# Hybrid decoder block on one core: tokens first in the load queue, lambda turned by TensorE, the order of the first tensor work changed

## The reference, cut to what matters

```python
def rms_norm(x, g):
    return x * lax.rsqrt(jnp.mean(x * x, -1, keepdims=True) + 1e-6) * g

h = jnp.concatenate([meta, x], axis=1)             # 272 x 1024
u = rms_norm(h, g_mix)
z = u @ w_in                                       # 1024 x 2048
c_val, c_gate, r_x, r_gate = jnp.split(z, 4, -1)   # 512 each
conv_out = conformer_conv_group(c_val, c_gate, ...)  # GLU, causal conv of 31 taps, LayerNorm, silu
lru_out = griffin_group(r_x, r_gate, ...)          # conv of 4 taps, RG-LRU, gelu gate
#   in rg_lru: log_a = -8 * r * softplus(-lam)     # lam: 512 values
h = h + concatenate([conv_out, lru_out]) @ w_out
u = rms_norm(h, g_ffn)
h = h + moe_ffn(u, ...)                            # 32 experts, top 4, clamped SwiGLU
out = rms_norm(h, g_final)[:, 16:]
```

## Time and profile before

| | us |
|---|---|
| median of 3 executions | 1006.41 |
| lowest, highest | 1006.39, 1010.56 |
| the profiled execution | 1006.83 |
| its span | 1005.0 |

### The profile page before, as it was taken

One profiled execution on the slowest core, in us unless ns is written; L12 is line 12 of the kernel. 1 busy time (PEld: TensorE's weight loads), 2 busy tenths in 40 slices (PEclk: granted clock), 3 DMA queues, 4 the chain that ended last, 5 costly groups with the idle time before them and its releaser, 6 DMA issues.

```text
span 1005.0 us, 11664 instructions
## 1 busy us (share of the span) xinstructions
PE 976.6 (97%) x4737; PEld 387.7 (39%) x4737; DVE 235.8 (23%) x624; ACT 163.0 (16%) x312; POOL 45.4 (5%) x89
## 2 busy tenths in 40 slices
PE   9999999999999999999999999999999999999996
PEld 7888433333343333333333333333333333333332
DVE  6986311112211111111111111111111111111121
ACT  5783211111101000111111101110011110100112
POOL 2860000000000000000000000000000000000000
PEclk9999999999999999999999999999999999999999
DMA  9999999999999999999999999999999999999995
GB/s 272 361 398 425 363 407 425 428 429 432 435 431 429 431 432 430 430 434 430 430 434 433 430 430 436 428 430 437 430 430 434 429 430 434 425 428 428 427 424 239
DMA packets 36802, 418.90 MB, mean 417 GB/s; under 512 B 5915, under 2 KB 16427, under 8 KB 19494
## 3 DMA queue, kind: packets, MB, share of 16 engines
q1 hardware_dynamic: 36038, 418.17, 98.9%
q10 hardware_dynamic: 736, 0.34, 0.1%
HBM read 417.45 MB, written 1.05 MB: 416 GB/s over the span
## 4 chain that ended last, share of the span: by engine, by line
PE 82%; DMA 14%; ACT 2%; another core or an unknown queue 1%; DVE 0%; issue 0%; SPq 0%; ACTq 0%; DVEq 0%
PE bank L1487 37%; PE bank L1532 19%; DMA gu_ring<-in_w_gate_up 10%; PE bank L1285 6%; PE bank L1459 5%; PE bank L1397 4%; DMA dn_ring<-in_w_down 4%; PE bank L1304 3%; PE bank L1391 3%; ACT reg L750 2%; PE bank L1508 1%; PE bank L1502 1%; PE bank L1224 0%; SPq L396 0%
## 5 line engine op out<-in xcount | busy, mean ns | idle before, releaser
L1487 PE MATMUL bank<-gu_ring,reg 128*64 128x512 f32 x2048 | 450.4, 595 | 11.1 <-DMA gu_ring<-in_w_gate_up 11.0
L1487 PEld LDWEIGHTS bank<-gu_ring,reg 128*64 128x64 f32 x2048 | 142.6, 137 | 310.1 <-issue 285.3
L1532 PE MATMUL bank<-dn_ring,reg 128*64 128x512 f32 x1024 | 227.4, 595 | 7.7 <-ACT reg L750 7.2
L1114 DVE TENSOR_SCALAR reg<-bank 128x256 f32<-128x256 f32 x64 | 24.2, 420 | 587.4 <-PE bank L1487 587.4
L1532 PEld LDWEIGHTS bank<-dn_ring,reg 128*64 128x64 f32 x1024 | 70.5, 137 | 143.0 <-issue 124.5
L745 ACT ACTIVATE reg<-reg 128x512 f32<-128x512 f32 x29 | 18.3, 630 | 456.4 <-DVE reg L1114 456.4
L1459 PE MATMUL bank<-reg 64*128 64x512 f32 x256 | 63.9, 616 | 0.9 <-DVE reg L1183 0.9
L1285 PE MATMUL bank<-dn_ring,gu_ring 128*128 128x272 f32 (+1 forms) x256 | 59.0, 390 | 0.3 <-ACT reg L612 0.3
L1397 PE MATMUL bank<-xh,reg 128*64 128x512 f32 x248 | 58.5, 592 | 0.0
L1285 PEld LDWEIGHTS bank<-dn_ring,gu_ring 128*128 128x128 f32 x256 | 48.4, 190 | 9.6 <-DMA gu_ring<-in_w_in 0.6
L752 ACT ACTIVATE reg<-bank 128x512 f32<-128x512 f32 x29 | 17.3, 597 | 208.4 <-PE bank L1532 208.4
(11 more groups left out here) (257 smaller groups left out, 424.7 us busy)
## 6 DMA issues: line engine op xcount, KB each, us to landing
gu_ring<-in_w_gate_up SPq DMA_DIRECT2D x46, 4096.0 KB, 33.0
dn_ring<-in_w_down SPq DMA_DIRECT2D x22, 4096.0 KB, 33.0
gu_ring<-in_w_gate_up SPq DMA_DIRECT2D x31, 2048.0 KB, 39.2
dn_ring<-in_w_down SPq DMA_DIRECT2D x10, 2048.0 KB, 20.3
dn_ring<-in_w_down SPq DMA_DIRECT2D x17, 1024.0 KB, 14.2
gu_ring<-in_w_gate_up SPq DMA_DIRECT2D x9, 1024.0 KB, 7.8
gu_ring<-in_w_in SPq DMA_DIRECT2D x6, 1024.0 KB, 12.3
dn_ring<-in_w_out SPq DMA_DIRECT2D x4, 1024.0 KB, 11.2
```

The lines of the kernel that those rows point to most:

```text
L1114: ins = V.tensor_scalar(half(xglu, b), glu_v[:, 0], 7.0, None, ALU.min)
L1487: ins = mm(gub[b][64 * h:64 * h + 64, :], xgT[:, j, :], of_half(gu_ring[:, s, j, 1024 * b:1024 * b + 1024], h), start=False, stop=(j == KD ...
L1532: ins = mm(out[64 * h:64 * h + 64, :], a[:, at:at + SLOTS], dn_ring[:, s, k, 512 * h:512 * h + 512], start=(i == 0), stop=(i == KD - 1))
```

## The change

SP no longer loads the identity: ACT does, as its first load, with a semaphore of its own. So the tokens are the first loads in SP's queue. `lam` is loaded as four rows of 128 into `grow`, which has 20 rows now, and is turned together with the gains; POOL reads its four columns from `colv` and waits for `g_ok`. PE issues six dummy products and not nine. It turns chunks 0 to 6 of the first token tile before it turns `grow`, and chunk 7 of the first tile and of the meta tokens just ahead of chunk 7 of the second tile. DVE squares the first token tile before it copies the turned gains. The two DVE operations for softplus go behind the eight `normed_x`. The vectors are turned after chunk 4 of `z_half(0, 0)` and not ahead of it, and chunk 0 of the first product waits for one DVE copy instead of two.

```diff
@@ -39,7 +39,7 @@
 
 V_CW, V_CB, V_LG, V_LB, V_LW, V_LCB, V_BA, V_BX = 0, 31, 32, 33, 34, 38, 39, 40
 NV = 41
-NG = 2 * KD
+NG = 2 * KD + CC
 GP = 4
 PK = KD // GP
 
@@ -134,7 +134,7 @@
         mixl = lnsq
         bdiag = xh[:, 0, :].rearrange("p (c n) -> p c n", c=2 * CC)
         prod = xh[:, 1, :].rearrange("p (i t) -> p i t", i=PROD)
-        lamc = tiny[:, 32:36]
+        lamc = colv[:, CC * NV + 2 * KD:CC * NV + NG]
         hsq = xh[:, :, :].rearrange("p b (d t) -> p (b d) t", d=4)
 
 
@@ -241,7 +241,7 @@
 
 
         x_in, meta_in = [sem("x_in0"), sem("x_in1")], sem("meta_in")
-        g_in, lam_in, vec_in, cst_in = sem("g_in"), sem("lam_in"), sem("vec_in"), sem("cst_in")
+        g_in, id_in, vec_in, cst_in = sem("g_in"), sem("id_in"), sem("vec_in"), sem("cst_in")
         tri_ok, selb_ok = sem("tri_ok"), sem("selb_ok")
         lruw_in, route_in, bgu_in = sem("lruw_in"), sem("route_in"), sem("bgu_in")
         win0_in, row3_in = sem("win0_in"), sem("row3_in")
@@ -333,7 +333,6 @@
         @block.sync
         def _(sp):
 
-            sp.dma_start(cst[:, C_ID:C_ID + P], const[:, C_ID:C_ID + P]).then_inc(g_in, 16)
             for t in range(TT):
                 sp.dma_start(xh[:, t, :], x[0, t * P:(t + 1) * P, :]).then_inc(x_in[t], 16)
             def win_single(p):
@@ -538,7 +537,7 @@
                 ins.then_inc(sp_pool, 1)
                 pool.wait_ge(sp_pool, done[0])
 
-            pool.wait_ge(lam_in, 16)
+            pool.wait_ge(g_ok, 1)
             after(G.tensor_scalar(spt[3], lamc, -1.0, 0.0, ALU.mult, ALU.max))
             after(G.tensor_scalar(spt[2], lamc, 0.0, None, ALU.max))
             after(G.tensor_tensor(spt[0], spt[3], spt[2], ALU.add))
@@ -593,10 +592,11 @@
         @block.scalar
         def _(act):
 
+            act.dma_start(cst[:, C_ID:C_ID + P], const[:, C_ID:C_ID + P]).then_inc(id_in, 16)
             act.dma_start(metah, meta).then_inc(meta_in, 16)
             for r, row in enumerate((g_mix, g_ffn)):
                 act.dma_start(grow[KD * r:KD * (r + 1), :], row[0].rearrange("(k n) -> k n", k=KD)).then_inc(g_in, 16)
-            act.dma_start(lamc, lam[0].rearrange("(c p) -> p c", p=P), allow_slow_non_contiguous=True).then_inc(lam_in, 16)
+            act.dma_start(grow[2 * KD:NG, :], lam[0].rearrange("(c n) -> c n", c=CC)).then_inc(g_in, 16)
 
             act.wait_ge(set_ok, 1)
             nc.scalar.activation(tiny[:, 38:39], one_col, ACT.Sqrt)
@@ -841,11 +841,11 @@
             V.memset(ssq[:, 2:3], 1.0).then_inc(set_ok, 1)
             v.wait_ge(set_ok, 1)
 
-            v.wait_ge(g_ps, 1)
-            V.tensor_copy(colv[:, CC * NV:], bank[7][:, 512 - NG:512]).then_inc(g_ok, 1)
             v.wait_ge(x_in[0], 16)
             V.tensor_tensor_reduce(out=sq_scr[:, 0:D], in0=xh[:, 0, :], in1=xh[:, 0, :], scale=1.0, scalar=0.0,
                                    op0=ALU.mult, op1=ALU.add, accum_out=ssq[:, 0:1]).then_inc(sq0_ok, 1)
+            v.wait_ge(g_ps, 1)
+            V.tensor_copy(colv[:, CC * NV:], bank[7][:, 512 - NG:512]).then_inc(g_ok, 1)
             def scaled_x(k):
                 v.wait_ge(xT_ps, k + 1)
                 V.tensor_scalar(xg[:, k, :], bank[k][:, 0:T], gcol(k), None, ALU.mult).then_inc(xT_dve, 1)
@@ -874,15 +874,15 @@
 
             v.wait_ge(rb_ps, 1)
             link(V.tensor_copy(rb, bank[3][:, 0:T]))
-            v.wait_ge(sp_act, 1)
-            link(V.tensor_scalar(spt[2], spt[1], 2.0, None, ALU.add))
-            V.reciprocal(spt[2], spt[2]).then_inc(sp_act, 1)
             normed_x(0)
             normed_x(1)
             v.wait_ge(zg_ps, 1)
             V.tensor_tensor(gate0, bank[1][:, 0:T], rb, ALU.mult).then_inc(sq0_ok, 1)
             for k in range(2, KD):
                 normed_x(k)
+            v.wait_ge(sp_act, 1)
+            link(V.tensor_scalar(spt[2], spt[1], 2.0, None, ALU.add))
+            V.reciprocal(spt[2], spt[2]).then_inc(sp_act, 1)
             v.wait_ge(vecT, 1)
             V.tensor_copy(colv[:, 0:CC * NV], bank[7][:, 0:CC * NV]).then_inc(vec_ok, 1)
             v.wait_ge(zg_act, 1)
@@ -1224,22 +1224,30 @@
                     mm(b[:, 0:P], ones[:, :], ones[:, :], start=True, stop=True)
 
             pe.wait_ge(set_ok, 1)
-            keep_busy(bank[6], 9)
+            keep_busy(bank[6], 6)
+
+            def x_turned(t, k):
+                return nc.tensor.transpose(bank[k][:, META + t * P:META + (t + 1) * P], xh[:, t, k * P:(k + 1) * P], ident)
+
+            def meta_turned(k):
+                return nc.tensor.transpose(bank[k][:, 0:META], metah[:, k * P:(k + 1) * P], ident[0:META, 0:META])
+
+            pe.wait_ge(id_in, 16)
+            pe.wait_ge(x_in[0], 16)
+            for k in range(KD - 1):
+                x_turned(0, k)
             pe.wait_ge(g_in, 48)
             nc.tensor.transpose(bank[7][:, 512 - NG:512], grow, ident[0:NG, 0:NG]).then_inc(g_ps, 1)
-            pe.wait_ge(x_in[0], 16)
-            for t in range(TT):
-                if t == TT - 1:
-                    pe.wait_ge(meta_in, 16)
-                    for k in range(KD):
-                        nc.tensor.transpose(bank[k][:, 0:META], metah[:, k * P:(k + 1) * P], ident[0:META, 0:META])
-                    pe.wait_ge(x_in[t], 16)
-                for k in range(KD):
-                    if t == 0 and k == KD - 1:
-                        pe.wait_ge(g_ok, 1)
-                    ins = nc.tensor.transpose(bank[k][:, META + t * P:META + (t + 1) * P], xh[:, t, k * P:(k + 1) * P], ident)
-                    if t == TT - 1:
-                        ins.then_inc(xT_ps, 1)
+            pe.wait_ge(meta_in, 16)
+            for k in range(KD - 1):
+                meta_turned(k)
+            pe.wait_ge(x_in[1], 16)
+            for k in range(KD):
+                if k == KD - 1:
+                    pe.wait_ge(g_ok, 1)
+                    x_turned(0, k)
+                    meta_turned(k)
+                x_turned(1, k).then_inc(xT_ps, 1)
 
             def spread_rstd():
 
@@ -1251,6 +1259,14 @@
                     ins = mm(bank[3][:, META + t * P:META + (t + 1) * P], rstd[:, t:t + 1].to_broadcast([P, P]), ident, start=False, stop=True,
                              is_transpose=True, skip_group_check=True)
                 ins.then_inc(rb_ps, 1)
+
+            def turn_vectors():
+
+                pe.wait_ge(vec_in, 16 * 9)
+                pe.wait_ge(xT_act, KD)
+                for c in range(CC):
+                    ins = nc.tensor.transpose(bank[7][:, c * NV:(c + 1) * NV], vrow[:, c * P:(c + 1) * P], ident[0:NV, 0:NV])
+                ins.then_inc(vecT, 1)
 
             def z_half(p, b):
                 first = b
@@ -1279,12 +1295,15 @@
                         if k % 2:
                             pe.wait_ge(xT_act, (1, 3, 4, 5)[k // 2])
                         else:
-                            pe.wait_ge(xT_dve, (2, 3, 4, 5)[k // 2])
+                            pe.wait_ge(xT_dve, (1, 3, 4, 5)[k // 2])
                     if p == 1 and first and k == 0:
                         pe.wait_ge(uT_ok, KD)
                     ins = mm(bank[2 * (p % 2) + b][:, t0:T], w[:, k, b, :], (uT if p else xg)[:, k, t0:], start=(k == 0), stop=(k == KD - 1))
-                    if p == 0 and first and k == 4:
-                        spread_rstd()
+                    if p == 0 and k == 4:
+                        if first:
+                            spread_rstd()
+                        else:
+                            turn_vectors()
                 if first:
                     ins.then_inc(zg_ps, 1)
                 else:
@@ -1305,12 +1324,6 @@
 
             for p in range(KD):
                 z_half(p, 1)
-                if p == 0:
-                    pe.wait_ge(vec_in, 16 * 9)
-                    pe.wait_ge(xT_act, KD)
-                    for c in range(CC):
-                        ins = nc.tensor.transpose(bank[7][:, c * NV:(c + 1) * NV], vrow[:, c * P:(c + 1) * P], ident[0:NV, 0:NV])
-                    ins.then_inc(vecT, 1)
                 if p == CC + 2:
                     pe.wait_ge(yc_ok, CC - 1)
                     mm(bank[4][:, 0:SEQ], ones[:, :], lnr, start=True, stop=True).then_inc(mean_ps, 1)
```

## The result

| | kernel before | changed kernel |
|---|---|---|
| median | 1006.91 (17 executions) | 1010.03 (17 executions) |
| lowest | 1005.93 | 1009.40 |
| highest | 1010.56, and one of 4251.99 | 1011.54 |
| profiled execution | 1006.83 | 1011.54 |
| its span | 1005.0 | 1009.6 |

The execution of 4251.99 us has no explanation here; with it or without it the median is the same within 0.02 us. The ratio is 1.0031, 95% interval 1.0025 to 1.0038: the change costs 3.1 us, from 2.5 to 3.8. By the bound that the prediction set itself, 0.5%, that is "same", but it is clear of the scatter, it is on the slow side, and it lies outside the range of 1005.0 to 1008.0 that was given. The question is where 3.1 us come from when 0.5 were expected back.

What follows compares the result with a forecast made beforehand. The expert weight stream bounds the kernel and follows PE's arrival at the first expert, 108 us. A first product 0.55 us earlier carries to the end, other parts 0: median 1006.41 becomes 1005.9, range 1005.0 to 1008.0.

Steps and rivals of the forecast that it cites:

- What bounds the kernel: Expert weight stream: its end follows PE's arrival at the first expert, 108 us, one for one.
- Six dummies end at 4.2: PE's start: twelve dummy records end at 4.22 us, against 5.50 for eighteen.
- The vectors' and softplus' new places: Vectors' turning inside `z_half(0, 0)` and softplus behind `normed_x`: same cost as before, 0 in the sum.
- the cover of 0.7 us: DVE before `glu`: vectors' copy and multiply end by 16.2 us, `glu` is due at 16.9, so the delay is hidden.
- The landings on ACT's queue: `grow`'s three loads: landing 2.6 to 4.6 us after issue, at 5.3 to 7.3 us, more likely 6.
- one of the signs that the prediction had named: PE idle before the turning of `grow`, its loads late: listed as showing the forecast wrong.
- The tokens' earlier issue: SP's queue: tokens issued at 0.72 us, not 1.16, 0.44 earlier; first tile to land at 4.4.
- The second tile: Second token tile: landing at about 5.95 us instead of 6.2, 0.25 gained, bounds none and 0.44.
- the gain of 0.55 us: First product at 8.1 us instead of 8.67, with the same gain at 108 us and at the end.
- The rival with 0.18: TensorE's clock rises late after a 0.2 us PE break at 4.2: 1006.8 to 1008.3, likeliest 1007.2; chance 0.18.
- Its sign: Clock rival's sign: weight loads of 280 ns or more in the tokens' turning beyond the first few.
- A delay of `w_in` by the single values: Lambda's 512 single values hold up `w_in`; without them its first piece lands at 6.9 to 7.9 us, not 8.3.

Runs made afterwards that it cites:

- e8: Kernel before with only the identity's load moved from SP's queue to the head of ACT's; 1011.26 us, ratio 1.0045.
- e5: Changed kernel with nine dummies, plus eight more between the first tile's turning and the wait for the rows; 1007.73 us, ratio 1.0008.
- e2: Changed kernel, six dummies, with the identity back at the head of SP's queue; 1008.41 us, ratio 1.0016.
- e10: Kernel before with only lambda loaded as four rows of the turned block; 1009.17 us, ratio 1.0016.
- e4: Changed kernel with the identity back at the head of SP's queue and nine dummies; 1006.74 us, ratio 1.0001.
- e7: Changed kernel with SP holding all of `w_in` until the first token tile has landed; 1009.3 us, one execution.
- e9: Changed kernel with ACT loading the rows of gains and lambda first, then identity, then meta tokens; 1010.94 us, ratio 1.0039.
- e11: Changed kernel with nine dummies and the identity as SP's second load, between the two token tiles; 1006.70 us, ratio 1.0000.
- e14: e11 with lambda as four columns again; 1006.11 us, ratio 0.9995.
- e3: Kernel before with only the dummies cut from nine to six; 1008.29 us, ratio 1.0013.
- e1: Changed kernel with nine dummies again, nothing else; 1009.80 us, ratio 1.0023.
- e12: e4 with three more dummy products behind the first tile's turning; 1007.23 us, ratio 1.0005.
- e13: e11 with six dummies instead of nine; 1009.07 us, ratio 1.0022.

## Why the prediction was wrong

**What bounds the kernel: right.** PE's lateness at the first expert went through to the end nearly one for one (4.74 us there, 4.6 in the span), by the hole that moved along. The other kernels follow less exactly: the ten records of e8 end 4.2 us later than before and its span is 3.5 longer, in e5 1.8 and 2.0, in e2 4.9 and 3.9, in e10 3.4 and 2.4. In the changed kernel and all fourteen experiments the two numbers lie within 1.2 us of each other.

**Six dummies end at 4.2: right** (4.22). **The vectors' and softplus' new places cost nothing: right.** Their turning costs 20.43 - 20.06 = 0.37 us, against 0.38. In e4, where nothing else is late, DVE still idles 0.93 us for PE ahead of `glu`:

```profile
17.70 0.44 DVE L896 TENSOR_TENSOR reg<-bank,reg 128x272 f32<-128x272 f32 x1 [0.93 <-PE bank L1301]
```

It had 1.12, so the cover of 0.7 us that I gave it was there.

**The landings on ACT's queue: the step that failed first.** I gave `grow` 2.6 to 4.6 us behind its issue, by the tokens' landings, though their row says 3.6 to 4.6 and the 2.6 is the meta tokens'. I took 6 us on the clock as likely, "since they are small", set 7.3 as the worst end, and dismissed it because no such small load landing so late had a row. Lambda was issued at 2.56 and let PE go 5.6 us later, at 8.2, behind an idle of 1.34 us, which is one of the signs that the prediction had named. The trace of the kernel before had a row that warns, for the same 2 KB as single values, also last in ACT's queue (L599, time from issue to landing):

```profile
DMA to landing us min/median/max: 5.8/5.8/5.8
```

There only POOL waited for it. As four rows with nothing else changed it let PE go 4.0 us behind its issue (e10), in the changed kernel 5.6; and the change put that landing ahead of PE's turning. In the DMA records of the changed kernel its four packets are moved between 7 and 8 us, the only ones of ACT's queue in that microsecond:

```profile
q10 hardware_dynamic: 4, 0.00, 0.5%
```

The meta tokens show the same. They landed 2.6 us behind their issue before; now (L596, time from issue to landing):

```profile
DMA to landing us min/median/max: 4.7/4.7/4.7
```

I had the numbers to see the danger: I counted the identity's and meta tokens' bytes as what they would take from the tokens, and never turned the question round, what the tokens' 1 MB would do to the identity. The identity had no term of its own in the sum, though every turning needs it: it landed at 5.0, 4.3 us behind its issue, when the first tile, expected at 4.4, had been there since 4.7. Size was no help to the small ones. The Trainium skill, DMA: Bandwidth & Descriptors, Queues, rings and completion order, says that each engine takes turns between queues packet by packet, and that the completion count lands behind every earlier write of that engine, across queues; by that a small load beside a megabyte on the other queue is late, and the traces of e7 to e9 agree in direction. No run here separates turn-taking from completion, and neither is all of it, since from 2 to 3 us the engines were not full. First the changed kernel, then the kernel before (the last numbers are granted clock, DMA share and GB/s):

```profile
2.00:3.00 1.00, 1.00 (x7) 1.00 (x7) 0.00 (x0) 0.01 (x1) 0.00 (x0) 1.00 0.44 125
2.00:3.00 1.00, 1.00 (x7) 1.00 (x7) 0.00 (x0) 0.43 (x1) 0.00 (x0) 1.00 1.07 258
```

By 3 us only twenty of ACT's packets had moved in the changed kernel. The share is 0.43 to 0.53 in all six kernels with the identity first on ACT's queue, e7 with its held `w_in` among them, and 0.89 to 1.07 in the six with it at the head of SP's. In the remaining four it is 0.52 to 0.83. What leaves the engines half idle there stays open. The tokens' earlier issue came to nothing as well: the first tile landed at 4.7, where it had been 4.8.

**The second tile: wrong way.** Expected at 5.95, 0.25 us earlier for 0.44 us of earlier issue. It landed 5.7 us behind its issue at 1.2, at 6.9. In e11, where the identity stands between the tiles, ACT starts on it at 6.45. Only in e9, where the identity was ACT's fourth load, did the tile come nearly as early as forecast, 4.6 us behind its issue, at 5.8. These are single profiled executions, and the landing scatters: with the identity at SP's head it was 6.2 in the kernel before, 6.9 in e4 and 7.9 in e2. So moving the identity aside is not shown to bring the tile forward at all. Of the gain of 0.55 us, 0.25 rested on the 5.95; the rest was to come from PE being ready earlier. It is: in e14 (product at 8.53) ACT's first copy follows its square at once, where it had waited 0.40 us.

```profile
6.62 1.06 ACT L607 ACTIVATE dn_ring<-xh 128x1024 f32<-128x1024 f32 x1 [1.31 <-DMA xh<-in_x]
...
7.68 0.47 ACT L610 ACTIVATE dn_ring<-bank,wrx 128x272 f32<-128x272 f32 x1
```

But the tile came 0.4 us later than in the kernel before. From ACT's start on it to the first product it is 1.91 us in e14, e4 and e12, and in e3 with the old order too: behind a late tile the order of turning decides nothing.

**The clock: seen, priced too low, and given too small a chance.** The rival with 0.18 was the mechanism that carried most of the loss: 3.2 of 4.74 us in the profiled execution, and with the clock kept up (e5, which also has nine dummies) the ratio falls from 1.0031 to 1.0008, with intervals that do not touch. Its condition, the break of 0.2 us at 4.2, was 0.89 us and followed by one of 1.34, since it was worked out with landings that were wrong. And I let it act once, before the rise. e1 shows a level that had risen and fell again, so a break behind the rise matters too. Its sign was set too high as well: I asked for weight loads of 280 ns or more in the tokens' turning, and at the low level they took 230, so the sign would have stayed silent. From e1 to e5 the products that kept the clock up gave 1.5 to 2.1 us. My highest value for it, 1008.3, would have fitted e3, with one of the causes, and e2, with two; the changed kernel has three.

**The parts do not add.** Alone on the kernel before, the identity's move costs 4.5 parts in a thousand, lambda's rows 1.6 and six dummies 1.3, 7.4 together; the whole change costs 3.1. Even the low ends of the three intervals add to 4.0, over the 3.8 that the whole may be. The likely reason is that they share one loss, the low clock until the first products are through, and the new turning order softens it: PE works on the first tile while the rows are late. With lambda as rows and nine dummies, the new order and the vectors' place turn 1.0016 (e10) into 1.0001 (e4); these intervals overlap a little, so the softening is likely and not more.

## What to carry to other kernels

Ahead of the first heavy work, ask of each wait what else stands on the DMA engines when that load is in flight, in both directions: a load that moves to a second queue does not leave the way, and a few rows issued behind a megabyte can land later than the megabyte. A load's landing in the old kernel is a row for the new one even where nobody waited for it. Dummy work that bridges to the first data should be sized by a late landing, not the mean one; a break of 0.58 us there (e10) went with a loss of 1.6 us. That more than nine would pay is not shown (e12). And where a clock rival rests on a gap, price it with the worst gap of every load concerned, and let it strike again after the rise.

## What the runs showed of the hardware

- One 64 KB load of 128 rows, issued at 0.72 us on the other queue, landed at 5.0 us, and at 3.3 at the head of SP's queue in e4 (2.6 us behind its issue). Issued at 2.03 us behind three row loads it landed at 7.5 (e9). The sixteen engines were busy for 0.44 of the microsecond from 2 to 3 us in the changed kernel and for 1.07 of it in the kernel before.
- TensorE's granted clock fell to 0.50, 1.2 GHz, at about 9.7 us in e1 while PE was at work, behind an idle of 1.15 us that had ended at 7.9; at 8.1 in e3, behind one of 1.09 that had ended at 7.8; and at 7.6 in e7, behind one of 1.08 that had ended at 7.3. Behind an idle of 1.05 us and another of 0.42 in e13 PE kept the high pace from 5.3 us on. With PE kept busy over the same time (e5) no low pace is seen behind 6.6 us.
- Times of one kernel spread by more than the effects studied here: over 4.3 us in e3 and 3.2 in e13, but also over 4.9 in the 32 executions of the kernel before timed beside e1 to e4. The Trainium skill, TensorE: Matmul & The Clock Gate, Part 1, says that the moment of the rise varies between runs of one kernel; the spreads would fit that, and would fit the tokens' landings too, which vary by 1.7 us between profiles of kernels that issue them alike (second tile, 6.2 to 7.9). Which executions were at which level can't be told from times alone, and one profile of each kernel is all there is.
- Lambda's 2 KB, the last load of ACT's queue, landed 5.8 us behind its issue as 512 single values in the kernel before and as four rows let PE go 4.0 us behind it in e10 and 5.6 in the changed kernel. A delay of `w_in` by the single values is not shown: with rows its first piece took 5.2 to 6.8 us to land (e7 aside), with columns 5.9 to 6.9.
